# A state space table moved from VectorE to GpSimd, and its scan pieces placed anew between the softmaxes

## The reference

```python
def first_block(x, c, ...):
    sh1, sc1, gt1, sh2, sc2, gt2 = jnp.split(c_act @ w_ada[l] + b_ada[l], 6, axis=-1)
    u = _modulate(h, g_mix[l], sh1, sc1)          # rmsnorm, scale, shift
    h = h + gt1 * _hybrid_mixer(u, ...)
    ...

def _hybrid_mixer(u, w_in, ...):
    proj = u @ w_in                               # q, k, v, us, g_att, g_ssm
    # three dilated windows per head, merged by their log-sum-exp
    y_att = o_att @ w_proj_att
    y_ssm = _s5_branch(us, ...) @ w_proj_ssm
    merged = sigmoid(g_att + gb_att) * y_att + sigmoid(g_ssm + gb_ssm) * y_ssm
    return merged @ w_out

def _s5_branch(u, ...):                           # x[t] = a * x[t-1] + B u[t], complex, diagonal
    mag = jnp.exp(lr * dt); ang = li * dt
    ab_re, ab_im = mag * jnp.cos(ang), mag * jnp.sin(ang)
    ...
    _, _, xr, xi = lax.associative_scan(combine, (a_re_t, a_im_t, bu_re, bu_im), axis=1)
    y = C_re xr - C_im xi + d_skip * u
    y = jax.nn.gelu(y)
    return y * jax.nn.sigmoid(y @ w_glu + b_glu)
```

## Time and profile before

| | us |
|---|---|
| median of 3 runs (2552.46 to 2554.11) | 2553.14 |
| the profiled execution | 2552.27 |
| its span, first to last instruction | 2550.4 |
| TensorE busy in the span | 2502.7 |
| VectorE busy | 1307.3 |
| GpSimd busy | 972.2 |
| ScalarE busy | 910.0 |

### The profile page before, as it was taken

How to read it: one execution, slowest core, us unless ns; L and a number is a source line. 1 busy time by engine, 2 the same in 40 slices (tenths; PEclk the granted TensorE clock), 3 DMA queues, 4 the chain that set the end, 5 groups by cost and what they waited for, 6 DMA issues and landing times.

```text
span 2550.4 us, 32843 instructions
## 1 busy us (share of the span) xinstructions
PE 2502.7 (98%) x11398; PEld 1987.4 (78%) x11398; DVE 1307.3 (51%) x1779; ACT 910.0 (36%) x1295; POOL 972.2 (38%) x384
## 2 busy tenths in 40 slices
PE   6999999999999999999999999999999999999998
PEld 3777667888788888677788888788887777788886
DVE  8856646356431338768531338531348768531344
ACT  3444424234422233554422233431333553421331
POOL 1332323444244443233344443344443233344443
PEclk8999999999999999999999999999999999999998
DMA  5222742322233232222133232233232222232232
GB/s 227 91 74 64 249 175 74 115 93 97 66 100 113 91 106 84 66 88 102 58 99 115 90 105 84 66 98 109 98 103 70 82 84 99 66 98 91 99 103 78
DMA packets 69702, 253.37 MB, mean 99 GB/s; under 512 B 8928, under 2 KB 11104, under 8 KB 68480
## 3 DMA queue, kind: packets, MB, share of 16 engines
q1 hardware_dynamic: 69632, 252.46, 29.6%
HBM read 244.76 MB, written 2.10 MB: 97 GB/s over the span
## 4 chain that ended last, share of the span: by engine, by line
PE 91%; DVE 5%; issue 3%; ACT 1%; DMA 0%; POOL 0%; SPq 0%; DVEq 0%; ACTq 0%; POOLq 0%
PE unit_bank L484 27%; PE unit_bank L485 27%; PE unit_bank L486 27%; PE score L571 2%; PE mix L627 1%; DVE x L1813 1%; DVE unit_bank L1811 1%; PE out_bank L607 1%; PE mix L676 1%; PE mix L526 1%; PE out_bank L532 1%; PE score L866 1%; PE mix L635 0%; DVE arena L1553 0%; PE out_bank L777 0%
## 5 line engine op out<-in xcount | busy, mean ns | idle before, releaser
L446 POOL TENSOR_TENSOR w_lo<-raw,w_hi 128x1024 fp32r<-128x1024 f32 (+2 forms) x376 | 967.0, 2572 | 1556.3 <-ACT w_hi L912 1556.3
L484 PE MATMUL unit_bank<-u_hi,w_hi 128*128 128x512 f32 x2160 | 850.4, 394 | 3.4 <-POOL w_lo L446 2.9
L912 ACT ACTIVATE w_hi<-raw 128x1024 fp32r<-128x1024 f32 (+2 forms) x376 | 416.9, 1109 | 1212.8 <-PE unit_bank L486 1173.7
L486 PE MATMUL unit_bank<-u_hi,w_lo 128*128 128x512 f32 x2160 | 841.7, 390 | 0.0
L485 PE MATMUL unit_bank<-u_lo,w_hi 128*128 128x512 f32 x2160 | 841.6, 390 | 0.0
L484 PEld LDWEIGHTS unit_bank<-u_hi,w_hi 128*128 128x128 f32 x2160 | 405.8, 188 | 112.3 <-issue 21.9
L486 PEld LDWEIGHTS unit_bank<-u_hi,w_lo 128*128 128x128 f32 x2160 | 405.8, 188 | 85.2
L485 PEld LDWEIGHTS unit_bank<-u_lo,w_hi 128*128 128x128 f32 x2160 | 405.9, 188 | 84.3 <-issue 1.9
L484 PE MATMUL unit_bank<-h_hi,w_hi 128*128 128x512 f32 x992 | 387.0, 390 | 0.5 <-DVE h_lo L1688 0.5
L486 PE MATMUL unit_bank<-h_hi,w_lo 128*128 128x512 f32 x992 | 385.9, 389 | 0.0
L485 PE MATMUL unit_bank<-h_lo,w_hi 128*128 128x512 f32 x992 | 385.9, 389 | 0.0
(11 more groups left out here) (311 smaller groups left out, 1944.0 us busy)
## 6 DMA issues: line engine op xcount, KB each, us to landing
raw<-in_w_gate_up SPq DMA_DIRECT2D x168, 512.0 KB, 3.5
raw<-in_w_down SPq DMA_DIRECT2D x64, 704.0 KB, 4.1
raw<-in_w_in SPq DMA_DIRECT2D x66, 512.0 KB, 3.5
raw<-in_w_up SPq DMA_DIRECT2D x30, 512.0 KB, 3.5
raw<-in_w_out SPq DMA_DIRECT2D x24, 512.0 KB, 3.5
f<-in_w_ada_rows SPq DMA_DIRECT2D x22, 512.0 KB, 4.5
raw<-in_w_down SPq DMA_DIRECT2D x16, 512.0 KB, 3.5
ada_late<-in_w_ada_rows SPq DMA_DIRECT2D x10, 512.0 KB, 4.5
```

The source lines that it names most:

```text
L446: e.tensor_tensor(w_lo[:, s, 0:n], raw[:, s, 0:n], as32(w_hi[:, s, 0:n]), ALU.subtract).then_inc(lo_ready, 1)
L484: e.matmul(bank[:], wh, hi(k), start=n == 0, stop=False)
L486: mm = e.matmul(bank[:], wl, hi(k), start=False, stop=last)
L912: e.activation(w_hi[:, s, 0:n], raw[:, s, 0:n], ACT.Copy).then_inc(hi_ready, 1)
```

## The change

It does three things. GpSimd makes the table of turns: columns 0 to 63 as soon as sine and cosine are there, ahead of its first w_lo, and the last doubling (columns 64 to 127, all tiles) behind the w_lo of pair 0; each instruction waits for the one before it through the semaphore `pool_step`, and DVE waits once for `turn_ready`. DVE grows C at once after the first unit's input, both parts together. The state space pieces become three per tile pair (`turned`, `scanned`, `turned_back`) and are placed by a small table: tile pair 0 is turned before head pair 0, one short piece stands after the third softmax step (n == 2) and the others behind the last copy of probabilities (n == 6); head pair 3 has none. `outputs(0)` and `outputs(1)` on TensorE and ACT's copies of them come one softmax step earlier.

```diff
+        angle = sb("angle", [P, 4, 8])
+        pool_step, turn_ready = sem("pool_step"), sem("turn_ready")
         @block.gpsimd
-            split_pairs(IN1, MERGE1 - IN1, D)
+            step = Steps(e, pool_step)
+            def tt(out, a, b, op):
+                step(e.tensor_tensor(out, a, b, op))
+            zr, zi, t1, t2 = (angle[:, n, :] for n in range(4))
+            def square_angle():
+                tt(t1, zr, zr, ALU.mult)
+                tt(t2, zi, zi, ALU.mult)
+                tt(zi, zr, zi, ALU.mult)
+                tt(zi, zi, zi, ALU.add)
+                tt(zr, t1, t2, ALU.subtract)
+            def double(n):
...
+                tt(p1, re, wide(zr), ALU.mult)
+                tt(p2, im, wide(zi), ALU.mult)
+                tt(turn[:, 0, :, n:2 * n], p1, p2, ALU.subtract)
+                tt(p1, re, wide(zi), ALU.mult)
+                tt(p2, im, wide(zr), ALU.mult)
+                tt(turn[:, 1, :, n:2 * n], p1, p2, ALU.add)
+            step(e.memset(turn[:, 0, :, 0:1], 1.0))
+            step(e.memset(turn[:, 1, :, 0:1], 0.0))
+            e.wait_ge(ssm_act, 2)
+            step(e.tensor_copy(zr, co[:, 8, :]))
+            step(e.tensor_copy(zi, co[:, 7, :]))
+            square_angle()
+            square_angle()
+            n = 1
+            while n < CHUNKS // 2:
+                double(n)
+                square_angle()
+                n *= 2
+            split_pair(IN1, D)
+            double(CHUNKS // 2)
+            e.sem_inc(turn_ready, 1)
+            split_pairs(IN1 + 1, MERGE1 - IN1 - 1, D)
         @block.tensor
-                    if j == HEAD_PAIRS - 1 and n:
-                        outputs(n - 1)
+                    if j == HEAD_PAIRS - 1 and n < 2:
+                        outputs(n)
         @block.scalar
-                    if last and n >= 2:
-                        e.wait_ge(y_done, n - 1)
+                    if last and n in (1, 2):
+                        e.wait_ge(y_done, n)
         @block.vector
             modulate(0, 0)
-            def squared(re, im):
...
-            while n < CHUNKS // 2:
-                double(n, 0, SSM_TILES, slot(23), slot(24))
-                squared(zr, zi)
-                n *= 2
             tt(t1, mag, mag, ALU.mult)
             tt(t2, t1, t1, ALU.mult)
             step(e.tensor_copy(decays[:], wide(t2, CHUNKS)))
             step(e.memset(decays[:, :, 0:1], 0.0))
+            grow(C_grown, STRIDE + 1, per_state("c_re"), per_state("c_im"), True)
+            e.sem_inc(C_ready, 1)
             settled()
+            e.wait_ge(turn_ready, 1)
             e.wait_ge(bu_ready, 4)
                 def turned():
-                    double(CHUNKS // 2, 2 * j, 2, p1, p2)
+                    if j:
+                        e.wait_ge(scan_ready, j)
...
                     step(e.tensor_tensor_scan(bi, r, p5, 0.0, ALU.mult, ALU.add))
+                def turned_back():
...
-                    if n < 4:
-                        tiles[n // 2]()
-                    elif j == 0:
-                        grow(C_grown, STRIDE + 1, per_state("c_re"), per_state("c_im"), True, (n // 2 - 2,), (4, 6))
-                        if n == 6:
-                            e.sem_inc(C_ready, 1)
+                    if n == 2 and j < 3:
+                        (tiles[0].scanned, tiles[1].turned_back, tiles[3].turned)[j]()
+                    if n == 6 and j == 0:
+                        tiles[0].turned_back()
+                        tiles[1].turned()
+                        tiles[1].scanned()
+                    if n == 6 and j == 1:
+                        tiles[2].turned()
+                        tiles[2].scanned()
+                        tiles[2].turned_back()
+                    if n == 6 and j == 2:
+                        tiles[3].scanned()
+                        tiles[3].turned_back()
+            tiles = [scan_parts(j) for j in range(HEAD_PAIRS)]
+            tiles[0].turned()
             for j in range(HEAD_PAIRS):
                 heads(j)
```

More of the change, by code:

```diff
@@ L15 @@
+from collections import namedtuple
 from contextlib import ExitStack
@@ L451, in split_pairs, with wide @@
                     split_pair(p0 + i, n)
-            split_pairs(IN1, MERGE1 - IN1, D)
+            step = Steps(e, pool_step)
[9 more added lines that the diff above has]
+            def double(n):
+                def wide(ap):
+                    return ap[:, :, None].broadcast_to([P, SSM_TILES, n])
+                re, im = turn[:, 0, :, 0:n], turn[:, 1, :, 0:n]
+                p1, p2 = (ssm_tmp[:, 2 * at:2 * at + 2, :].rearrange("p a k -> p (a k)")[:, 0:8 * n].rearrange(
+                    "p (i c) -> p i c", c=n) for at in range(2))
+                tt(p1, re, wide(zr), ALU.mult)
[20 more added lines that the diff above has]
+            split_pairs(IN1 + 1, MERGE1 - IN1 - 1, D)
             split_pairs(MERGE1, DC // 2, 6 * P)
@@ L1068, in heads @@
                                      stat_bank[0:32, :], ACT.Copy).then_inc(k_taken, 1)
-                    if last and n >= 2:
-                        e.wait_ge(y_done, n - 1)
-                        e.activation(y_chunk[:, 4 * n - 8:4 * n - 4, :].rearrange("p i k -> p (i k)"), stat_bank[:],
+                    if last and n in (1, 2):
+                        e.wait_ge(y_done, n)
+                        e.activation(y_chunk[:, 4 * n - 4:4 * n, :].rearrange("p i k -> p (i k)"), stat_bank[:],
                                      ACT.Copy).then_inc(y_taken, 1)
@@ L1400, in _, with grow @@
                 tt(li_at(n + m), t1, t2, ALU.add)
-            def grow(out, n, re, im, conj, parts=(0, 1), scratch=(21, 23)):
+            def grow(out, n, re, im, conj):
                 def many(ap):
@@ L1410, in grow @@
                 p1, p2 = (arena[:, at * T:at * T + 128 * n].rearrange("p (i m c) -> p i m c", i=SSM_TILES, m=n)
-                          for at in scratch)
-                for part in parts:
+                          for at in (21, 23))
+                for part in range(2):
                     tt(p1, many(re), power(part), ALU.mult)
@@ L1500, in _ @@
             step(e.memset(decays[:, :, 0:1], 0.0))
+            grow(C_grown, STRIDE + 1, per_state("c_re"), per_state("c_im"), True)
+            e.sem_inc(C_ready, 1)
             settled()
+            e.wait_ge(turn_ready, 1)
             e.wait_ge(bu_ready, 4)
+            Tile = namedtuple("Tile", ("turned", "scanned", "turned_back"))
             def scan_parts(j):
@@ L1528, in scanned @@
                     e.tensor_tensor(bi, p3, p4, ALU.add).then_inc(scan_ready, 1)
-                return turned, scanned
+                return Tile(turned, scanned, turned_back)
             def split_out(j):
@@ L1563, in take_probs @@
                         pT_ready, 1)
-                tiles = scan_parts(j)
                 for h in range(2):
```

## The result

| | before | after |
|---|---|---|
| median of 13 runs, us | 2552.96 (2550.88 to 2554.11) | 2558.11 (2554.42 to 2560.45) |
| span of the profiled execution, us | 2550.4 | 2556.3 |

The ratio is 1.002, with a 95% interval of 1.0012 to 1.0029: some 5 us slower. The forecast was 2557.5 us.

What follows compares the result with a forecast made beforehand. TensorE, busy 98% of the span, was taken as the bound, so other engines count only where it waits. Terms -5.6 + 9.7 + 0.5 = +4.6 us gave a median of 2557.5 us, range 2550 to 2564.

Steps and rivals of the forecast that it cites:

- the loss at the start: TensorE's first pair, with the table on GpSimd: ends at 63.8 instead of 54.1, 9.7 us lost.
- the gain: Head pairs: TensorE's eight waits for scaled probabilities (4.4 us) and one for the scan (1.2) go, 5.6 us in all.
- The 0.5 for growing C: After the first pair: a DVE instruction growing C can hold up the w_lo TensorE waits for, 0.5 us lost.
- the 0.30: GpSimd's table chain: assumed fixed time per instruction in us, 78 of them, plus 6.7 us for columns, 30 us.
- the line: GpSimd instruction price from two recorded forms: 2.22 ns a column and 0.13 us fixed.
- the last input is ready at 62.4: First pair's input on DVE, delayed by GpSimd's w_lo and last doubling; TensorE then needs 1.4 us, ending at 63.8.
- rival 3: Longer GpSimd chain or code load: w_lo sets TensorE's start; 2564.5 us at 0.45 fixed, 2558 to 2560 with load; chance 0.22.
- the held-up input: First pair's 16 DVE input instructions: GpSimd's last doubling holds up six of them, 7.6 us.
- rival 1: GpSimd's small steps are cheap, fixed part 0.20 us or less: start loses 5.7 us, about 2554 us; chance 0.15.
- rival 2: DVE gets in between GpSimd's instructions, first pair ends within 1 us of before: 2548 to 2549 us; chance 0.13.
- The code load: First call to loaded GpSimd code, behind the wait for sine: some 6 us by the skill, some 2 us more overall.
- rival 4: Short pieces after the third softmax step meet a w_lo, bringing back 4.4 us of waits: 2562 us; chance 0.03.

Runs made afterwards that it cites:

- the last doubling on DVE: Changed kernel with the table's last doubling moved from GpSimd to DVE after growing C, chain to column 63 kept: 2556.44 us, ratio 1.0016 to the kernel before.
- twenty more steps: Changed kernel plus twenty unused 8-column squarings at the end of GpSimd's chain, ahead of w_lo: 2568.48 us, ratio 1.0063 to the kernel before.

## Why the prediction was right

- **The sign and the size** are right (+4.6 forecast, +5.2 measured), but as a sum of two terms that were both too small: the loss at the start, 9.7, was 13.1, and the gain, 5.6, was 7.7. The 0.5 for growing C was not there. That the errors of +3.4 and -2.1 leave so little between them is luck; the sign, with a loss larger than the gain, is not.
- **The chain on GpSimd.** Predicted end 41.6, measured 48.1. A step of 8 columns alone is 0.29 us apart (the ten squarings) and 0.33 in the doublings, so the 0.30 held. Two things were mis-sized: a doubling of 256 columns took 1.07 us a step (38.27 to 44.67) where the line gives 0.87 with the 0.30, and the squarings beside DVE took up to 2.6 times as long (3.43 us against 1.32); against 1.40 us for five, the groups at 17.53, 28.84, 36.34 and 44.67 lost 5.3 us together. The prediction priced what GpSimd costs DVE and gave what DVE costs GpSimd no term of its own in the chain. By the length of the whole chain the fixed part came to 0.38 ((36.4 - 6.7) / 78). "The loss hardly depends on my 0.30" does not fit the prediction's own figures, 5.7, 9.7 and 12.7 us for 0.20, 0.30 and 0.40.
- **What sets TensorE's start and end.** The step that failed is "the last input is ready at 62.4". It was ready at 55.65, since w_lo came when 13 of the 16 were through, and TensorE, which takes it chunk by chunk, never waited for it. TensorE was bound by w_lo at 53.71, by the arm of the prediction given for a fixed part of 0.40 (w_lo ready at 54.3, a loss of 12.7). So the mechanism that set the time is rival 3's, and the forecast's own, the held-up input, did not set it. (The prediction's w_lo "ready at 47" is by its own terms 41.6 + 4.7 + 1.4 = 47.7.) The pair's own length, taken as 12.5, was 13.5 at the lower clock; over all runs it was 11.4 to 13.7. The experiments with the last doubling on DVE and with twenty more steps show that w_lo alone sets it. The price of a collision, "each holding up one DVE instruction, 7.6 us", is 3.5 us where it was measured by itself (six GpSimd instructions, five DVE ones lengthened).
- **Growing B.** "About as much" in collisions as before is wrong: it lost 0.3 us where it had lost 3.7, and B was turned before TensorE wanted it.
- **The gain in the head pairs.** All eight waits and the scan's went, as said. The term was too small because it counted the idle time alone: around each of them the turns of the two heads run one after the other instead of together. Turn to turn around the stall of head pair 0 it was 9.45 us and is 7.38 (before, then after):

```profile
104.86 0.55 PE L766 MATMUL mix<-tabs,arena 128*128 128x128 f32 x3 [0.36 <-ACT arena L1044]
105.63 0.55 PE L766 MATMUL mix<-tabs,arena 128*128 128x128 f32 x3 [0.23 <-ACT arena L1044]
```

```profile
117.24 0.82 PE L813 MATMUL mix<-tabs,arena 128*128 128x128 f32 x6
124.62 1.04 PE L813 MATMUL mix<-tabs,arena 128*128 128x128 f32 x8
```

- **Which part made the gain** the prediction did not ask. In head pair 0 either part is enough: the doubling taken out with the old places (33.3 us) or the new places with the doubling kept (33.4). In head pair 2 it is the doubling taken out (41.8 with the old places, 44.0 with the new places alone). In head pair 3 it is mostly the places, 1.1 of 1.5 us.
- **The w_lo of the next pairs.** 0.5 us was given to growing C. Pair 1's wait is 2.90 as before; pair 2's new 1.18 us stands behind a transfer (ACT idle 9.38 us before its w_hi), which the lower clock hid before (pair 1 took 12.6 us at 0.87 before, and takes 11.2 at 1.00 now, so it ends before pair 2's w_lo is there). That is argued from the profile and not tested.
- **The rivals.** The long chain (rival 3) had the right mechanism: w_lo sets the start. Its condition, a fixed part of 0.45, was not needed for that. Cheap steps (rival 1, 0.20 or less) and a hidden start (rival 2) are out: the steps were 0.29 us apart at the least, and the first pair ended 13.1 us later. The code load did not show. The short pieces after the third softmax (rival 4) met no stall.

## What to carry to other kernels

An engine that seems idle has a deadline when the critical engine next asks something of it: count the serial steps that fit before it, and cut the moved work there. Here the 20 us of GpSimd's chain up to column 15 (11.7 to 31.8) cost at most 1.2 us at TensorE's start, in a kernel 8 us faster, while with the whole chain it was 5 us slower. A long dependent chain on GpSimd must be priced twice, alone and beside DVE. And when a stall goes, the gain is read from mark to mark on the critical engine, not from its idle time.

## What the runs showed of the hardware

- A GpSimd instruction of 8 columns with two inputs took 0.2 to 0.25 us and followed the one before it, on whose end it waited, after 0.29 to 0.33 us; where DVE worked with two SBUF inputs most of the time, groups of five or more took 0.55 to 0.72 us a step.
- GpSimd instructions of 8 to 64 columns cost DVE nothing that shows (1.42 us for two of 512 columns; 0.75 for one, beside the 25 squarings), those of 256 columns lengthened some to 0.98 to 1.21 us, and beside larger ones a DVE instruction lasted as long as they did (1.4 to 1.5 us beside 1.4, 5.49 for two beside two w_lo of 5.28). In these rows the engine with the shorter instructions pays.
- The loading instruction on GpSimd's queue behind the wait, recorded with 11 ns at 12.1, left no pause between the copy and the first multiply (12.17 to 12.25).
